# Layer 0's mixer gates: two rows transposed, stored and broadcast by DMA in place of sixteen matrix products, and three output items taken block by block behind the norm

## What is computed

```python
yl = even_mixer(hl, *ew)      # u = h @ w_in; cat(conformer_conv(u[:1024]), pool_mix(u[1024:])) @ w_out
yc = even_mixer(hc, *ew)      # the context tokens
xl = xl + mod_l[:, 2] * yl    # the mixer's gate: one row of 1024 values for the latents,
xc = xc + mod_c[2] * yc       # one for the context
```

## Time and profile before

| | |
|---|---|
| median of 3 runs | 908.37 us (907.8 to 908.73) |
| the profiled execution | 905.56 us, span 903.9 us |
| PE busy | 827.9 us (92%) |
| DVE busy | 392.3 us (43%) |
| ACT busy | 166.5 us (18%) |
| POOL busy | 165.1 us (18%) |
| mean granted clock of TensorE | 0.981 |
| DMA | 293.46 MB, mean 325 GB/s |

### The profile page before, as it was taken

One profiled execution on the slowest core, in us unless ns is written; L12 is line 12 of the kernel. 1 busy time (PEld: TensorE's weight loads), 2 busy tenths in 40 slices (PEclk: granted clock), 3 DMA queues, 4 the chain that ended last, 5 costly groups with the idle time before them and its releaser, 6 DMA issues.

```text
span 903.9 us, 9965 instructions
## 1 busy us (share of the span) xinstructions
PE 827.9 (92%) x3683; PEld 367.7 (41%) x3683; DVE 392.3 (43%) x809; ACT 166.5 (18%) x445; POOL 165.1 (18%) x195
## 2 busy tenths in 40 slices
PE   4899999999979999988888999999899999978886
PEld 2444445445723333322227544546546333322222
DVE  1369999403533143332225486757635122212111
ACT  2301113203400000000014232337512000000000
POOL 2100094122121022221003243210220000000000
PEclk9899999999999999999999999999999999999999
DMA  8999446672997999999987438482486999999994
GB/s 362 410 420 377 188 186 279 267 293 78 348 389 289 387 403 424 427 420 426 423 342 325 175 105 309 162 356 90 197 365 232 390 425 422 426 422 429 423 426 170
DMA packets 28414, 293.46 MB, mean 325 GB/s; under 512 B 5134, under 2 KB 5488, under 8 KB 9668
## 3 DMA queue, kind: packets, MB, share of 16 engines
q1 hardware_dynamic: 23472, 283.25, 76.5%
q0 software_dynamic: 4752, 9.38, 3.0%
q10 hardware_dynamic: 132, 0.04, 0.0%
HBM read 289.74 MB, written 8.94 MB: 330 GB/s over the span
## 4 chain that ended last, share of the span: by engine, by line
PE 61%; DMA 18%; DVE 15%; issue 2%; ACT 1%; POOL 1%; SPq 1%; DVEq 0%; POOLq 0%; ACTq 0%
PE bank L1379 20%; DMA ring<-in_gu_pack 14%; DVE WORK L2402 10%; PE bank L1404 10%; PE bank L511 8%; PE bank L1538 5%; DMA ring<-in_win_pack 3%; PE bank L1239 3%; PE bank L1485 2%; PE bank L1321 1%; DMA hT<-x_rows,smalli 1%; PE bank L1388 1%; PE bank L578 1%; PE bank L605 1%; PE bank L569 1%
## 5 line engine op out<-in xcount | busy, mean ns | idle before, releaser
L1379 PE MATMUL bank<-ring,WORK 128*64 128x512 f32 x352 | 106.4, 621 | 11.5 <-DMA ring<-in_gu_pack 7.1
L1379 PE MATMUL bank<-ring,hT 128*64 128x512 f32 x368 | 110.3, 606 | 2.8 <-DMA ring<-in_gu_pack 2.8
L2402 DVE SCALAR_TENSOR_TENSOR WORK<-WORK,par 128x512 f32<-128x512 f32 x116 | 90.7, 859 | 0.0
L511 PE MATMUL bank<-ring,hT 128*128 128x512 f32 (+2 forms) x256 | 88.1, 499 | 0.7 <-ACT hT L1658 0.7
L1404 PE MATMUL bank<-ring,WORK 128*64 128x512 f32 x384 | 87.8, 601 | 0.6 <-ACT WORK L1700 0.6
L2280 DVE SCALAR_TENSOR_TENSOR WORK<-WORK,bank 128x256 f32<-128x256 f32 x16 | 7.7, 480 | 139.6 <-ACT WORK L1695 139.6
L2280 DVE SCALAR_TENSOR_TENSOR hT<-hT,WORK,bank 128x256 f32<-128x256 f32 x18 | 8.6, 480 | 132.1 <-ACT hT L1695 126.4
L1700 ACT ACTIVATE WORK<-bank 128x256 f32<-128x256 f32 x34 | 13.0, 383 | 268.0 <-PE bank L1388 268.0
L511 PEld LDWEIGHTS bank<-ring,hT 128*128 128x128 f32 x256 | 46.1, 190 | 36.5 <-issue 34.2
L1485 PE MATMUL bank<-hT,ring 128*128 128x512 f32 x128 | 58.9, 620 | 1.8 <-DMA ring<-in_win_pack 1.8
L1538 PE MATMUL bank<-ring,B 128*128 128x512 f32 x128 | 56.2, 594 | 0.0
(11 more groups left out here) (347 smaller groups left out, 1210.3 us busy)
## 6 DMA issues: line engine op xcount, KB each, us to landing
ring<-in_gu_pack SPq DMA_DIRECT2D x41, 2048.0 KB, 16.1
ring<-in_mod_pack SPq DMA_DIRECT2D x24, 2048.0 KB, 8.7
ring<-in_down_pack SPq DMA_DIRECT2D x21, 2048.0 KB, 25.2
WORK<-in_gu_pack SPq DMA_DIRECT2D x5, 2048.0 KB, 21.8
ring<-in_wout_pack SPq DMA_DIRECT2D x4, 2048.0 KB, 8.9
ring<-in_win_pack SPq DMA_DIRECT2D x3, 2048.0 KB, 36.9
X<-in_gu_pack SPq DMA_DIRECT2D x3, 2048.0 KB, 8.6
B<-in_gu_pack SPq DMA_DIRECT2D x3, 2048.0 KB, 22.6
```

The costliest lines, as they stand in the source:

```text
L511: mm = pe.matmul(dst[:, 0:hi - lo], hT[:, k, t * P:(t + 1) * P], w[:, k, :], start=k == 0, stop=k == KC - 1)
L1379: mm = pe.matmul(dst[ST * x:ST * x + ST, :], HG[L][s][:, k, :], columns(units[x], 512 * k, 512), start=k == 0, stop=k == KC - 1)
L2402: ins = dve.scalar_tensor_tensor(out=acc, in0=src, scalar=w, in1=acc, op0=ALU.mult, op1=ALU.add)
```

## The change

The sixteen gate products are replaced by two transposes of the gate columns into 8 partitions of bank 0. ScalarE copies them (8x256) to `GT_A` and stores them to a new tensor in memory, `gd_a`, of 2 x 1024 values. GpSimd waits for the last pool product (whose matrices share memory with `GB`) and for the store, then loads each row into `GB`, broadcast over 128 partitions. VectorE's `add_out` of layer 0 waits for these loads in place of ScalarE's copies. Item 2's blocks 0 to 3 move ahead of the wait for `conv_done`. Modulation products 6 and 7 follow each other between the transposes, and ScalarE copies both ahead of its work on the normed blocks. Behind the norm, items 0, 1 and 2 take block 4 each, then block 5 each, and so on to 7, and the turns of products 6 and 7 come behind all three. The counts of the semaphores follow.

```diff
+        gd_a = nc.dram_tensor("gate_rows_a", (2, D), F32, kind="Internal").ap()
...
+        GT_A = hw[0:8, 2048:2304]
...
         def gates_before(tag):
-            return {"a0": 0, "r0": 4, "a1": 5, "m1": 7}[tag]
+            return {"a0": 0, "r0": 1, "a1": 2, "m1": 4}[tag]
...
-            def gates(tag, L, v, streams, banks):
-
-                n = 0
-                for s in streams:
-                    for h in range(2):
-                        for c in range(4):
-                            mm = pe.matmul(bank[banks[n]][:, c * P:(c + 1) * P],
-                                           mods[:, L, v, 4 * h + c, s:s + 1].to_broadcast([P, P]), ident, start=True, stop=True)
-                        mm.then_inc(sem("gate_mms"), 1)
-                        n += 1
+            def turn_pair_gates():
+
+                for s in range(2):
+                    mm = pe.transpose(bank[0][0:8, P * s:P * s + P], mods[:, 0, 2, :, s], ident)
+                mm.then_inc(sem("gate_mms"), 1)
...
-            gates("a0", 0, 2, (0, 1), (0, 1, 2, 3))
+            turn_pair_gates()
...
             out_half(1, range(4))
+            out_half(2, range(4))
             pe.wait_ge(sem("conv_done"), 4)
-            pe.wait_ge(sem("gate_rows"), 4)
+            pe.wait_ge(sem("gate_rows"), 1)
             for t in range(NT):
                 for m in range(4):
                     mm = pe.transpose(bank[t][:, m * P:(m + 1) * P], CV[:, m, t * P:(t + 1) * P], ident)
                 mm.then_inc(sem("ln_turned"), 1)
-            out_half(2, range(4))
             mod_multiply(6)
+            mod_multiply(7)
             pe.wait_ge(sem("ln_rows"), 4)
...
-            mod_multiply(7)
-            for i in range(8):
+            for k in range(4, KC):
+                pe.wait_ge(sem("mix_done"), k - 3)
+                for i in range(3):
+                    mm = out_half(i, (k,))
+                    if k == KC - 1:
+                        mm.then_inc(sem("out_mm"), 1)
+            mod_turn(6)
+            mod_turn(7)
+            for i in range(3, 8):
                 if i >= 3:
                     pe.wait_ge(sem("out_used"), i - 2)
                     out_half(i, range(4))
                 for k in range(4, KC):
-                    if i == 0:
-                        pe.wait_ge(sem("mix_done"), k - 3)
...
                 mm.then_inc(sem("out_mm"), 1)
-                if i == 0:
-                    mod_turn(6)
-                    mod_turn(7)
...
-            gate_rows("a0", (0, 1), (0, 1, 2, 3))
+            act.wait_ge(sem("gate_mms"), 1)
+            act.activation(GT_A, bank[0][0:8, 0:256], ACT.Copy).then_inc(sem("gate_rows"), 1)
+            act.wait_ge(sem("gate_rows"), 1)
+            act.dma_start(gd_a.rearrange("s (k f) -> k s f", k=8), GT_A.rearrange("k (s f) -> k s f", s=2)).then_inc(sem("gates_stored"), 16)
             mod_copy(6)
+            mod_copy(7)
             for m in range(4):
...
-            mod_copy(7)
...
-            act.wait_ge(sem("gates_stored"), 32)
+            act.wait_ge(sem("gates_stored"), 48)
...
-                dve.wait_ge(sem("gate_mms"), gates_before(f"a{L}") + (4, 2)[L])
+                if L == 0:
+                    dve.wait_ge(sem("mod_turned"), 8)
+                else:
+                    dve.wait_ge(sem("gate_mms"), gates_before("a1") + 2)
...
-                dve.wait_ge(sem("gate_rows"), gates_before(f"a{L}") + 2 * len(streams))
+                if L == 0:
+                    dve.wait_ge(sem("spread_in"), 32)
+                else:
+                    dve.wait_ge(sem("gate_rows"), gates_before("a1") + 2)
...
-                    dve.wait_ge(sem("spread_in"), 96)
+                    dve.wait_ge(sem("spread_in"), 128)
...
+            pool.wait_ge(sem("pool_mm"), 8)
+            pool.wait_ge(sem("gates_stored"), 16)
+            for s in range(2):
+                pool.dma_start(GB[:, s, :], gd_a[s].partition_broadcast(P)).then_inc(sem("spread_in"), 16)
             pool.wait_ge(sem("ln_stats"), NT)
...
-            pool.wait_ge(sem("gates_stored"), 32)
+            pool.wait_ge(sem("gates_stored"), 48)
```

## The result

The changed kernel takes 911.87 us in the median of 5 runs (908.02 to 913.4), the kernel before 908.37 (905.84 to 909.19): a ratio of 1.0046, 95% interval 1.0026 to 1.0066, or +2.4 to +6.0 us. A second set of 6 runs gave 913.88 against 907.47 us, ratio 1.0072 (1.0054 to 1.0091). The medians differ by 3.5 us in the first set and by 6.4 us in the second: the change makes the kernel slower. (The ratios on record are not the quotients of the two medians, which is 1.0039 in the first set.) The profiled execution took 909.96 us (span 908.3), 4.4 above the one before.

A forecast was written before the change was run, and what follows sets the result against it. TensorE was taken to bound the stage from 156.05 us, VectorE's convolution taps before that. +2.05, less the moved 3.44, plus 0.7, 0.9 and 1.75 gave +2.0 us: 910.4 us against 908.37, range 907.8 to 912.8.

The forecast's parts named there:

- The case I gave 0.56: The whole kernel: the main forecast, slower by +1.2 to +2.8 us, some 0.36 of its chance beyond 1.8 us.
- rival (a): Pool products: the new 2.1 us pause halves TensorE's clock, 1.8 us lost, time 912.2 us; chance 0.12.
- Step 1: Gate rows before the pool products: of 3.5 us taken off TensorE, only 1.2 arrive; the fourth product waits for GpSimd.
- Step 2: Item 2's first half, ahead of the convolution wait: the convolution transposes begin at 158.1 instead of 156.05, +2.05 us.
- Steps 3, 4 and 5: New TensorE waits: before modulation product 7 +0.7 us, before the first mixed row's product +0.9, before item 3 +1.75.
- Step 6: The gate store and broadcast loads: loads land by 172.5 us, VectorE wants the rows at about 184; cost nothing.
- The sum's ends: Start of item 3: the summed shift of +2.0 us was given as +1.0 with all low ends, +2.8 with all high.
- Rival (b): Later stages: half-clock stretches behind waits ending at 437.7 and 868.3 us fall away, 908.6 or 906.8 us; chance 0.17.
- Rival (c): Waits at the first mixed row and item 3: covers better than seen, only +0.4 us, 908.8; chance 0.08.
- (d): Gate products: on the path after all, as pooled groups end earlier without them; 2.1 us come back, 908.3; chance 0.07.

The follow-up runs named there:

- turns_first: The changed kernel with the turns of modulation products 6 and 7 moved ahead of the last halves of items 0 to 2: 909.37 us, ratio 1.0026 to before.
- order_only: The kernel before with the new order alone, the sixteen gate products kept: 911.77 us, ratio 1.0038 to before.
- gates_only: The kernel before with the narrow gate rows alone (two transposes, store, broadcast loads), its order kept: 910.75 us, ratio 1.0019 to before.
- woven: The changed kernel with two of item 2's first four blocks moved between modulation products 6 and 7, and the turns ahead of the items: 906.56 us, ratio 0.9998.
- gates_again: The kernel before with the narrow gate rows alone, a second time: 909.05 us, ratio 1.0023 to before.
- before_again: The kernel before itself, unchanged, a second time: 907.47 us, ratio 0.9998.
- filled: The changed kernel with unread identity products in three pauses (before the modulation columns' wait, the fourth pool product and item 3): 910.01 us, ratio 1.0018 to before.
- filled_item3: The changed kernel with seven unread identity products in the pause ahead of item 3 alone: 910.65 us, ratio 1.0047 to before.
- item_by_item: The changed kernel with items 0, 1 and 2 taken one after the other behind the norm, turns still behind all three: 913.63 us, ratio 1.0066 to before.
- woven_filled: The `woven` kernel with unread identity products in the pauses ahead of the pool products: 907.65 us, ratio 1.0004 to before.
- turns_again: The `turns_first` kernel a second time: 910.09 us, ratio 1.0023 to before.
- after_again: The changed kernel itself, a second time: 913.88 us, ratio 1.0072 to before.

## Why the prediction was right, and where it was not

The sign held, and so did the mechanism of the sum: the moved work uncovers waits one by one. The size did not. The case I gave 0.56, +1.2 to +2.8 us, came in neither set's medians (+3.5, whose interval reaches down to +2.4, and +6.4); the forecast of 910.4 was 1.5 us short of the first. The range, 907.8 to 912.8, held the first set's 911.87 because it had room for a halved clock, to which I had given 0.12; the second set's +6.4 us lie beyond its upper end, +4.4. That rival (a) alone gave 912.2, close to 911.87, is partly luck, as shown below. By steps:

**Step 1** (1.2 us arrive of 3.5): about right without the halved clock, 1.06 measured; with it 0.11 arrive. The pause has two parts, though, 1.39 and 0.49 us in `turns_first`, and not the one of 2.1 ahead of the fourth product. I had the first three pool products start as soon as the gate transposes are through; they wait 1.39 us for ScalarE's modulation columns, which the gate products had covered. As a wait it costs nothing, since with the clock whole GpSimd's fourth group still decides.

**Step 2** (+2.05): stage A of `turns_first`, with the clock whole, is 17.24 against 15.19, +2.05.

**Steps 3, 4 and 5** (0.7, 0.9, 1.75): 0.72, 0.95 and 1.74 in the brackets above. B with the clock whole is 37.09 against 36.86, +0.2, where the sum had -0.1. `order_only` and `turns_first` show that these waits come from the order: where the turns stand first, two of the three are gone.

**Step 6** (nothing): the store was landed by 153.2, when the first load was issued, the loads landed within 5.2 us of their issue, and VectorE's first product with a gate, 30 us later, waited for none of them.

**The sum's ends** were added up wrongly. 2.05 less the moved 3.44 plus the low ends 0.6, 0.5 and 1.0 is +0.7 us, not +1.0; plus the high ends 1.0, 1.4 and 2.0 it is +3.0, not +2.8. The middle, +2.0, is right.

**The step that was mis-sized** is rival (a). I gave a halved clock 0.12 and looked for it at the pool products alone, as 1.8 us. It cost 0.95 us there in both profiles of the changed kernel, less than the 1.8, since the slower products run partly through the wait for GpSimd's fourth group (it came in six of the nine profiles that have this pause bare), and I missed that item 3's pause, 1.74 us behind the turns, could do the same: 1.5 us in one profile and 3.05 in the other. In the first profile the two make 2.4 us where (a) had 1.8, so its 912.2 came near by another sum. Without the halved clock the stage is 54.3 (17.24 + 37.09), +2.3 us, near my sum of +2.0; with it 56.75 and 58.33. The runs with identity products show it in stage time; in the medians it is less sharp. My argument against, that the new pause is shorter than those that had cost something, failed: 1.39 and 1.74 us are shorter than the 2.76 of the earlier trace rows and were followed by the halved clock all the same.

**Rival (b)**, halved stretches that fall away later, did not come: the changed kernel's profile has both stretches that I named, at 440 and 873 us. The later stages do scatter: the rest runs from 711.0 to 718.5 us over the fourteen profiles. The kernel before alone gave 711.0 and 714.6, the second with a halved stretch near 600 us that the first did not have. Rival (c) is out, since the three covers failed within 0.05 us of their cost. So is (d): in the changed profile GpSimd's fourth group ends 5.95 us after the mark (143.93 + 1.61 less 139.59), before it was 5.91.

**What stays open.** `gates_only` and `turns_first` have a stage no longer than before, or hardly, and are 0.2% slower, each in two sets. `woven`, with the same narrow rows, is not. The profiles show where most of the scatter of the rest comes from. I add up, over windows of one microsecond, how long TensorE's granted clock stood at 0.50 behind the gate transposes and up to TensorE's last product:

| about, us at 0.50 | kernels with the rest in us |
|---|---|
| 24 | before 711.0, woven 713.0 |
| 31 | changed 712.0, gates_again 714.6, turns_first 714.7 |
| 34 | before_again 714.6, filled 715.5, filled_item3 714.0, item_by_item 715.6 |
| 38 | order_only 715.1, woven_filled 715.0, turns_again 717.1 |
| 41 | gates_only 718.5, after_again 717.1 |

The rest grows with the halved time, which fits the halved clock as the cause of most of the scatter. Only `before`, `before_again` and `order_only` have no narrow rows. In their three lines of the table the kernels with narrow rows lie 0.4 to 2.0 us above them in the mean, so a small cost of the narrow rows behind the stage is neither shown nor excluded. Nor is it shown whether they bring on more halved stretches: without them the profiles have 24, 34 and 38 us, with them 24 to 41.

## What to carry to other kernels

Moving work out of a stage's cover is not free even where TensorE's total falls: the removed products had filled a wait for another engine, and the moved ones had covered a copy, a norm and a column. List for each moved piece what it hid, and put the pieces on which another engine waits (here the turns) ahead of the pieces on which none does; that alone was worth 3.1 us of stage time (the totals, 0.2% above the kernel before in place of 0.5 and 0.7%, point the same way). And cost every new pause of TensorE twice, as the pause and as a possible stretch at half clock behind it.

## What the hardware showed that I had not expected

The halved clock came with pauses of only 1.39 to 1.75 us. Behind item 3's pause of 1.74 us it stood at 0.50 in all four profiles that have it bare (both of the changed kernel, `order_only`, `item_by_item`); ahead of that pause TensorE did small turns, 16 records of 4 columns in 1.84 us. In the kernels with identity products in this pause it never fell. It is not the length of the pause alone: at the pool products the same pause was followed by it in six profiles of nine, and in the expert stage a pause of 3.21 us cost nothing in the first profile of the kernel before, while in its second profile the pause at the same place, 3.83 us there, was followed by a clock of 0.50 from 407.2 us.

The Trainium skill ("TensorE: Matmul & The Clock Gate", section "HAM oscillation — how this bites in real kernels") warns of idle gaps longer than those here. The runs show shorter ones followed by the same halved clock, at 0.8 to 0.95 us of stage time at the pool products and 1.5 to 3.05 us at item 3, and products that nobody reads, put into these pauses, took the loss away.
